# Output projection of a two-layer hybrid trunk: inputs and weight loaded earlier, three input slots, a new order of small steps

## The chip, the cores and the metric

The kernel runs on one core of one Trainium2 chip. The metric is the device time of one launch in microseconds, the median of several executions. All data are float32.

## The reference

A trunk of two layers is applied to 128 prompt rows and 1024 sample rows (1152 rows of 1024 features, nine tiles of 128 rows). One layer is:

```
xm   = rms_norm(x) * (1 + sc1) + sh1
proj = xm @ w_in                       # queries, keys, gates of three mixers
o    = concat(attention, gated linear attention, gated delta rule)
       # forward + backward scan, rms_norm per head * gain, times silu(z)
y    = o @ w_out                       # the output projection
x    = x + g1 * rms_norm(y, nrm1)
xm   = rms_norm(x) * (1 + sc2) + sh2
aff  = softmax(xm @ w_router)          # 16 experts, expert choice
x    = x + g2 * rms_norm(experts(xm, aff))
```

The change is about the lines from `y` to `aff`, and about how the stage ahead of them (the scans and the attention) ends.

## The kernel before, in words

The program is a chain of stages, and each stage ends with a barrier over all engines: `front` (projection by w_in, keys, convolution), `scan` (the two scans and the attention, interleaved by hand), `mixer_output` (output projection, residual, routing), `experts`. Each of the two layers runs all four. SBUF tensors and semaphores belong to a stage; only `B.x`, the masks and a few tables live throughout.

`mixer_output` (L2083) works through nine tiles, software pipelined, each engine with its own loop over t. For tile t:

- SP loads the three parts of the heads' output and the gates (`load(t)`, L2123) into one of two slots, and stores the normalised rows (L2150). Ahead of the loop it issues tile 0, the 4 MB of w_out in four pieces (L2135), tile 1, the branch gates, the residual rows of three tiles at a time (L2142) and w_router.
- DVE, `head_sums` (L2287 to L2292): forward plus backward, squares, sums per head, times z. `head_norms` (L2298 to L2302): times the gain, times the scale per head, which POOL works out (L2168, L2170) in between. The gain is scaled once (L2363) as soon as it has landed.
- PE, `turn_o` (L2224): eight transposes into the two halves of `ring`; ACT copies each half to `oT` (L2211). `project` (L2247): 16 products of 128 x 512 into `acc`; the trace shows each as two records.
- ACT, `branch_square` (L2192) sums the squares of `acc`; POOL makes the scale; DVE, `residual` (L2326, L2328) adds the branch to x; ACT, `row_square` (L2202); POOL; DVE, `normalise` (L2336) writes `xhat`.
- PE, `turn_x` (L2236): eight transposes of `xhat` into the same two halves of `ring`; DVE, `modulate` (L2311): eight products with scale and shift from `ring` to `xT`, four for each half. PE, `route` (L2256): the products with w_router, 16 columns wide, into the one bank `lg`. DVE, `largest` (L2341, L2343): the row maximum of `lg`, negated; ACT, the exponential (L2205); DVE, `affinity` (L2348 to L2354); PE and DVE turn it (L2262, L2376).

Two things set the order around the change. First, `ring` is shared: `turn_o(t)` waits for each half until `modulate(t - 3)` has read it. Second, each engine runs its program in order. PE's order in one pass of its loop is

```
for t in range(-3, TILES + 3):
    if t in (-2, -1): project(t + 2)
    if t >= 1 and has(t + 1): project(t + 1)
    if has(t - 3): turn_affinity(t - 3)
    if has(t): turn_x(t)
    if has(t - 1): route(t - 1)
    if has(t + 3): turn_o(t + 3)
```

and DVE's order in one pass is modulate(t-1), residual(t), head_sums(t+3), normalise(t), head_norms(t+3), largest(t-2), affinity(t-2), copy of affinity t-3. So modulate(t-1) follows turn_x(t-1), and largest(t-2) follows route(t-2); both of these stand in PE's pass t-1, route behind turn_x.

In `scan`, the last values of the delta rule's inverse are used by `values` (L1258). After that come four steps of the state, each with attention between, while SP only stores results (L1094). At that time the tensors Rk, TT, PM, NB, Tb and qk are no longer read.

Of the kernel before, what the change touches and what calls it, by code (L numbers as in the profile page):

```python
# [22 lines left out]
P = 128  # L23
# [153 lines left out]
def front(nc, T, B, l):  # L177
# [32 lines left out]
    with stage(nc, "front", l) as st:  # L210
        keysT, values = st.sb("keysT", [P, H_MLA, KEYS * P]), st.sb("values", [P, H_MLA, KEYS, VD])
        xmT = st.sb("xmT", [P, KD, ROWS])
        w = st.sb("w", [P, 2, KD, 512])
# [6 lines left out]
        wc = st.sb("wc", [P, 2, 3, 512])  # L220
# [713 lines left out]
CH = 64  # L934
# [4 lines left out]
def scan(nc, T, B, l):  # L939
# [30 lines left out]
    with stage(nc, "scan", l) as st:  # L970
        beta, la = st.sb("beta", [P, 2, 32]), st.sb("la", [P, 2, 32])
        qk = st.sb("qk", [P, 4, 2 * DQ])
        v = st.sb("v", [P, 2, 4, H, GK])
        Rk = st.sb("Rk", [P, 32, GK])
        kend = st.sb("kend", [P, 2, 32, GK])
        kq = st.sb("kq", [P, 3, 16, P])
        PM = st.sb("PM", [P, 32, CH])
        A = st.sb("A", [P, 2, 32, CH])
        TT = st.sb("TT", [P, 32, CH])
        nwT = st.sb("nwT", [P, 2, 2, 8, CH])  # L980
        NB = st.sb("NB", [P, 32, 32])
        Tb = st.sb("Tb", [P, 32, 32])
# [53 lines left out]
        s_out = st.sem("s_out")  # L1036
# [11 lines left out]
        with st.block() as block:  # L1048
            @block.sync
            def _(sp):  # L1050
# [70 lines left out]
                load_v(1)  # L1121
                for k in range(-1, GROUPS):
# [959 lines left out]

def mixer_output(nc, T, B, l):  # L2083
# [3 lines left out]
    with stage(nc, "mixer", l) as st:  # L2087
        wout = st.sb("wout", [P, KD, D])
# [3 lines left out]
        o = st.sb("o", [P, 2, D])  # L2092
        ob, z = st.sb("ob", [P, 2, W3]), st.sb("z", [P, 2, W3])
# [12 lines left out]
        c_in, w_in, r_in, gate_in = (st.sem(x) for x in ("c_in", "w_in", "r_in", "gate_in"))  # L2106
        t_in, stored = ([st.sem(f"{x}{i}") for i in range(2)] for x in ("t_in", "stored"))
# [12 lines left out]
        with st.block() as block:  # L2120
            @block.sync
            def _(sp):
                def load(t):  # L2123
                    s, r = t % 2, t * P
                    q = proj_row(t)
                    if t >= 2:
                        sp.wait_ge(o_p, 2 * (t - 2) + 3)
                    for dst, src in ((o[:, s, 0:256], T["mla_out"][r:r + P, :]), (o[:, s, 256:], T["scan_f"][r:r + P, :]), (ob[:, s], T["scan_b"][r:r + P, :]),
                                     (z[:, s, 0:GQ], T["proj"][q:q + P, C_GZ:C_DQ]), (z[:, s, GQ:], T["proj"][q:q + P, C_DZ:C_DB])):
# [11 lines left out]
                for g in range(3):  # L2141
                    sp.dma_start(B.x[:, 3 * g:3 * g + 3, :], xs[:, 3 * g:3 * g + 3, :]).then_inc(x_in[g], 16)  # L2142
                    if g < 2:
                        load(g + 2)
                    if g == 0:
                        sp.dma_start(wr[:], T["w_router"][l].rearrange("(k p) n -> p k n", p=P)).then_inc(r_in, 16)
                for t in range(0, TILES):
                    if t >= 0:
                        sp.wait_ge(xhat_v, t + 2)
                        sp.dma_start(T["xhat"][t * P:(t + 1) * P, :], xhat[:, t % 2]).then_inc(stored[t % 2], 16)  # L2150
                    if 2 <= t + 4 < TILES:
                        load(t + 4)
# [33 lines left out]
            def _(act):  # L2186
# [6 lines left out]

                for t in range(-3, TILES + 2):
# [19 lines left out]
            def _(pe):  # L2214
                def turn_o(t):
                    pe.wait_ge(o_v, t + 2)
                    for i in range(2):
# [4 lines left out]
                        for k in range(4):  # L2222
                            c = (4 * i + k) * P
                            mm = pe.transpose(ring[:, i, k, :], o[:, t % 2, c:c + P], B.ident)  # L2224
# [38 lines left out]

                for t in range(-3, TILES + 3):
# [14 lines left out]
            def _(dve):  # L2279
# [3 lines left out]
                def head_sums(t):  # L2283
                    s = t % 2
# [608 lines left out]
```

## Time and profile before

| | us |
|---|---|
| median of three runs | 4474.08 |
| lowest and highest run | 4464.86, 4477.98 |
| the profiled execution, its own time | 4473.7 |
| its span | 4471.9 |
| output projection stage, layer 0, first instruction to last product of affinity | 1140.7 to 1343.3 |
| the same, layer 1 | 3339.1 to 3541.5 |

Times in rows are microseconds from the start of the span. A row of a timeline gives start, duration, engine, line, operation, what it writes and reads, and in brackets how long the engine was idle before and what it waited for. PE rows of one kind that follow one another are drawn together (x32), and ends of matmuls are modelled. PE is TensorE's product, PEld its weight load, DVE VectorE, ACT ScalarE, POOL GpSimd; a name with q (SPq, ACTq) is the issue of a transfer. PEclk is the clock that TensorE was granted: 1.00 is 2.4 GHz, 0.50 is 1.2 GHz.

### The profile page before, as it was taken

How to read it: one execution, taken by the hardware profiler on the slowest of the kernel's cores; microseconds unless marked ns; L12 is line 12 of the kernel's file. 1: busy time of each engine (PE TensorE's matmuls, PEld its weight loads, DVE VectorE, ACT ScalarE, POOL GpSimd, SP SyncE). 2: the span in 40 equal slices, each digit the busy share in tenths (PEclk: the TensorE clock that was granted, in tenths of full speed). 3: DMA queues.
4: the chain of work that ended last, by engine and by line, in shares of the span. 5: the costliest groups of instructions: out<-in, count | busy, mean ns of one | idle time of the engine just before them, and what ended most of it. 6: DMA issues, size and time to landing. Idle time of an engine off the chain costs nothing. (4 is left out here: it accounts for less than half of the span.)

```text
span 4471.9 us, 80289 instructions
## 1 busy us (share of the span) xinstructions
PE 3865.3 (86%) x33620; PEld 3008.3 (67%) x33620; DVE 2161.6 (48%) x4904; ACT 973.8 (22%) x1962; POOL 1057.2 (24%) x1092
## 2 busy tenths in 40 slices
PE   4999968888795999999779998787869689999994
PEld 3444546676455999999744444566654389999994
DVE  3335045656455445544453440556646554445444
ACT  2233134444110000000033331444431100000001
POOL 0036034453220110001040450454522100110003
PEclk9999978888897999999989998888889789999997
DMA  7556353331516888888564652334224378888885
GB/s 265 170 189 245 128 129 77 80 69 36 182 68 235 296 279 283 283 292 291 173 231 152 242 195 64 95 82 97 53 74 168 117 254 280 294 280 283 284 289 174
DMA packets 557877, 836.17 MB, mean 187 GB/s; under 512 B 85864, under 2 KB 403368, under 8 KB 551372
## 3 DMA queue, kind: packets, MB, share of 16 engines
q1 hardware_dynamic: 471884, 711.08, 49.0%
q10 hardware_dynamic: 70432, 81.03, 5.4%
q0 software_dynamic: 15200, 38.94, 3.5%
q8 instruction: 266, 4.36, 0.4%
q14 instruction: 95, 0.78, 0.1%
HBM read 698.83 MB, written 132.10 MB: 186 GB/s over the span
## 5 line engine op out<-in xcount | busy, mean ns | idle before, releaser
L2545 PE MATMUL ffn_hb<-ffn_xT,ffn_w 128*128 128x144 f32 x8192 | 1058.9, 289 | 26.8 <-DMA ffn_w<-in_w_e 20.3
L2545 PEld LDWEIGHTS ffn_hb<-ffn_xT,ffn_w 128*128 128x128 f32 x8192 | 1029.5, 192 | 29.0 <-DMA ffn_w<-in_w_e 20.5
L521 PE MATMUL front_acc<-front_w,front_xmT 128*128 128x512 f32 (+2 forms) x2304 | 883.5, 544 | 21.3 <-DVE front_xmT L782 17.7
L521 PEld LDWEIGHTS front_acc<-front_w,front_xmT 128*128 128x128 f32 x2304 | 441.2, 194 | 449.5 <-issue 418.1
L2553 PE MATMUL ffn_acc<-ffn_hT,ffn_w 128*128 128x144 f32 x4096 | 547.3, 287 | 0.0
L2553 PEld LDWEIGHTS ffn_acc<-ffn_hT,ffn_w 128*128 128x128 f32 x4096 | 518.5, 190 | 6.7 <-issue 6.7
L2592 ACT ACTIVATE ffn_en<-ffn_hb 128x144 f32<-128x144 f32 x256 | 74.3, 290 | 1457.1 <-PE ffn_hb L2545 1457.1
L2475 POOL DMA_INDIRECT ffn_xe<-scratch_xhat,ffn_g_idx x34 | 34.4, 1012 | 1453.6 <-DVEq L2657 1399.1
L2702 DVE TENSOR_TENSOR ffn_hT<-ffn_en,ffn_hb 128x144 f32<-128x144 f32 x256 | 77.8, 304 | 607.6 <-ACT ffn_en L2592 607.2
L2247 PE MATMUL mixer_acc<-mixer_wout,mixer_oT 128*128 128x512 f32 x576 | 256.4, 604 | 3.2 <-DMA mixer_wout<-in_w_out 1.7
L2618 DVE TENSOR_SCALAR_CACHE_REDUCE ffn_junk<-ffn_row,ffn_pair 128x128 f32<-128x128 f32 (+2 forms) x324 | 245.3, 757 | 1.4
L1798 POOL TENSOR_TENSOR scan_prod<-scan_Tb,scan_NB 128x30 f32<-128x30 f32 (+5 forms) x300 | 181.6, 605 | 222.0 <-POOLq L1815 199.3
L2247 PEld LDWEIGHTS mixer_acc<-mixer_wout,mixer_oT 128*128 128x128 f32 x576 | 110.8, 195 | 136.7 <-issue 132.3
L591 POOL TENSOR_TENSOR x_res<-x_res,front_wc 128x1536 f32<-128x1536 f32 x18 | 72.1, 4003 | 550.6 <-DMA x_res<-scratch_proj 550.6
L2617 DVE TENSOR_SCALAR_CACHE_REDUCE ffn_junk<-ffn_row,ffn_pair 128x128 f32<-128x128 f32 (+6 forms) x252 | 187.2, 743 | 4.4
L1351 PE MATMUL scan_ring<-x_res 128*128 128x512 f32 (+1 forms) x400 | 160.0, 533 | 12.1 <-ACT x_res L1655 4.5
L1800 POOL TENSOR_TENSOR scan_Tb<-scan_Tb,scan_prod 128x30 f32<-128x30 f32 (+5 forms) x300 | 163.1, 544 | 23.5
L1962 DVE TENSOR_REDUCE scan_top<-x_res 128x1 f32<-128x1152 f32 (+1 forms) x72 | 88.7, 1232 | 146.1 <-ACT x_res L1659 127.8
L1332 PE MATMUL scan_ring<-x_res 128*128 128x64 f32 x1168 | 141.1, 275 | 0.9 <-ACT x_res L1682 0.9
L1332 PEld LDWEIGHTS scan_ring<-x_res 128*128 128x128 f32 x1168 | 138.7, 195 | 1.4 <-ACT x_res L1682 1.2
L1351 PEld LDWEIGHTS scan_ring<-x_res 128*128 128x128 f32 x400 | 68.7, 198 | 96.9 <-ACT x_res L1655 48.2
L649 ACT ACTIVATE front_out<-front_acc 128x512 f32<-128x512 f32 (+1 forms) x90 | 49.7, 552 | 386.1 <-PE front_acc L521 386.1
(332 smaller groups left out, 5108.8 us busy)
## 6 DMA issues: line engine op xcount, KB each, us to landing
ffn_w<-in_w_e SPq DMA_DIRECT2D x384, 1024.0 KB, 9.4
x_res<-in_w_mod SPq DMA_DIRECT2D x40, 1024.0 KB, 5.5
x_res<-scratch_proj SPq DMA_DIRECT2D x36, 768.0 KB, 6.1
scratch_proj<-front_out ACTq DMA_DIRECT2D x90, 256.0 KB, 2.2
ffn_row<-scratch_affT SPq DMA_DIRECT2D x36, 576.0 KB, 4.5
front_w<-in_w_in ACTq DMA_DIRECT2D x8, 2048.0 KB, 13.2
scan_qk<-scratch_qkv SPq DMA_DIRECT2D x16, 1024.0 KB, 9.9
scratch_qkv<-x_res SPq DMA_DIRECT2D x18, 768.0 KB, 3.5
```

The source lines that it names most:

```text
L521: mm = pe.matmul(acc[:, U % 2, 0:size], xmT[:, k, t * P:(t + 1) * P], w[:, n % 2, k, 0:size], start=k == 0, stop=k == KD - 1)
L1332: mm = pe.matmul(b[:, P:P + VD], probT[:, k * P:(k + 1) * P], kv[:, h % 2, KEYS_W + (j0 + k) * VD:KEYS_W + (j0 + k + 1) * VD], start=k == ...
L1351: mm = pe.matmul(ring[:, i % 2, 0:size], qT[:, n % 4, :], kv[:, h % 2, k0 + at:k0 + at + size], start=True, stop=True)
L1798: pool.tensor_tensor(x, wide(Tb[:, 0:i, i], n), NB[:, i + 1:32, i].unsqueeze(1).to_broadcast([P, i, n]), ALU.mult).then_inc(own, step())
L1800: pool.tensor_tensor(Tb[:, 0:i, i + 1:32], Tb[:, 0:i, i + 1:32], x, ALU.add).then_inc(own, step())
L1962: dve.tensor_reduce(top[:, c], prob[:, n % 2, 0:w], AX.X, ALU.max).then_inc(own, step())
L2247: mm = pe.matmul(acc[:, t % 2, n * 512:(n + 1) * 512], oT[:, t % 2, k, :], wout[:, k, n * 512:(n + 1) * 512], start=k == 0, stop=k == KD - 1)
L2545: mm = pe.matmul(hb[:, b, i * CAP:(i + 1) * CAP], w[:, r, k, c:c + P], xT[:, s, k, :], start=k == 0, stop=k == KD - 1)
L2553: mm = pe.matmul(part(c), w2[:, r, j % WIDTH, c * P:(c + 1) * P], hT[:, b, :], start=j == 0 and c % PER_BANK == 0, stop=j == KF - 1, skip_ ...
L2617: dve.tensor_scalar(junk[:, 0:a - lo], row[:, lo:a], mine, 0.0, ALU.is_ge, ALU.add, accum_out=counts[:, t, 0:1]).then_inc(own, step())
L2618: dve.tensor_scalar(junk[:, a - lo:hi - lo], row[:, a:hi], mine, 0.0, ALU.is_gt, ALU.add, accum_out=counts[:, t, 1:2]).then_inc(own, step())
L2702: dve.tensor_tensor(hT[:, b, :], en[:, b], hb[:, b, CAP:2 * CAP], ALU.mult).then_inc(h_done, 1)
```

## The change

- Two SBUF tensors live throughout the program: `B.late` (8192 numbers a partition) and `B.early` (4096). The weight slots of `front` and Rk, TT, PM, NB, Tb of `scan` move into `B.late`; `wc` of front and `qk` of scan into `B.early`. In `mixer_output`, `wout` is `B.late`, and the first of three input slots is `B.early`.
- SP issues the five loads of tile 0 and the four of w_out in `scan`, ahead of the stores of the last group, once PE has made the last `values`. The scan's SP waits for them at its end.
- `load(t)` has three slots: tiles 1 and 2 are issued at the stage's begin, tile t+5 behind the store of tile t.
- PE begins the stage with nine products of constants, 128 x 512 each, into `acc`.
- ACT: the row square of tile 0 stands in pass -1, ahead of the copies of tile 2.
- DVE: `largest` stands at the head of the pass, ahead of `modulate`; the sums of tile 0 stand ahead of the wait for the gain; the scaling of the branch gates stands at the end of pass -1 and no longer in residual(0).
- PE's loop (the order given above) is not touched.

```
+                def load_next():
+                    sp.wait_ge(head_out[0], 17)
...
+                    sp.wait_ge(od_out[0], 33)
+                    sp.wait_ge(od_out[1], 33)
+                    sp.wait_ge(og_out[0], 33)
+                    sp.wait_ge(u_p, 10)
+                    o, ob, z = mixer_inputs(B)
+                    q = proj_row(0)
+                    for dst, src in ((o[:, 0:256], T["mla_out"][0:P, :]), (o[:, 256:], T["scan_f"][0:P, :]), (ob, T["scan_b"][0:P, :]),
+                                     (z[:, 0:GQ], T["proj"][q:q + P, C_GZ:C_DQ]), (z[:, GQ:], T["proj"][q:q + P, C_DZ:C_DB])):
+                        sp.dma_start(dst, src).then_inc(next_in, 16)
+                    wo = T["w_out"][l].rearrange("(k p) n -> p k n", p=P)
+                    for i in range(0, KD, 2):
+                        sp.dma_start(B.late[:].rearrange("p (k n) -> p k n", k=KD)[:, i:i + 2], wo[:, i:i + 2]).then_inc(next_in, 16)
                 for k in range(-1, GROUPS):
                     g = k + 1
+                    if g == GROUPS:
+                        load_next()
                     if k >= 0:
                         for m in range(2):
                             store_gdn(k, m)
...
                 sp.wait_ge(s_out, 129)
+                sp.wait_ge(next_in, 16 * 9 + 1)
...
+def mixer_inputs(B):
+    return B.early[:, 0:D], B.early[:, D:D + 768], B.early[:, D + 768:D + 2 * 768]
...
-        wout = st.sb("wout", [P, KD, D])
+        wout = B.late[:].rearrange("p (k n) -> p k n", k=KD)
-        o = st.sb("o", [P, 2, D])
-        ob, z = st.sb("ob", [P, 2, W3]), st.sb("z", [P, 2, W3])
+        o, ob, z = ([x, more[:, 0], more[:, 1]] for x, more in zip(mixer_inputs(B), (
+            st.sb("o", [P, 2, D]), st.sb("ob", [P, 2, W3]), st.sb("z", [P, 2, W3]))))
...
-                    s, r = t % 2, t * P
+                    s, r = t % 3, t * P
-                    if t >= 2:
-                        sp.wait_ge(o_p, 2 * (t - 2) + 3)
+                    if t >= 3:
+                        sp.wait_ge(o_p, 2 * (t - 3) + 3)
...
-                load(0)
-                wo = T["w_out"][l].rearrange("(k p) n -> p k n", p=P)
-                for k in range(0, KD, 2):
-                    sp.dma_start(wout[:, k:k + 2], wo[:, k:k + 2]).then_inc(w_in, 16)
                 load(1)
+                load(2)
...
-                        load(g + 2)
+                        load(g + 3)
...
-                    if 2 <= t + 4 < TILES:
-                        load(t + 4)
+                    if t + 5 < TILES:
+                        load(t + 5)
...
+                def row_square(t):
+                    act.wait_ge(x_v, t + 2)
+                    act.activation(sq[:, 1], B.x[:, t, :], ACT.Square, accum_out=rs[:, t % 2, 1:2]).then_inc(x_a, 1)
                 for t in range(-3, TILES + 2):
                     s = t % 2
                     if t == -1:
                         branch_square(0)
-                    if has(t):
-                        if t:
-                            branch_square(t)
-                        act.wait_ge(x_v, t + 2)
-                        act.activation(sq[:, 1], B.x[:, t, :], ACT.Square, accum_out=rs[:, s, 1:2]).then_inc(x_a, 1)
+                        row_square(0)
+                    if t >= 1 and has(t):
+                        branch_square(t)
+                        row_square(t)
...
                 def project(t):
                     pe.wait_ge(oT_a, 2 * t + 3)
-                    if t == 0:
-                        pe.wait_ge(w_in, 65)
...
+                for _ in range(9):
+                    pe.matmul(acc[:, 1, 0:512], B.ident, B.masks[:].rearrange("p k c -> p (k c)"), start=True, stop=True)
...
+                def branch_gates():
+                    dve.wait_ge(gate_in, 49)
+                    for c in range(2):
+                        dve.scalar_tensor_tensor(gate[:, c, :], gate[:, c, :], float(D) ** 0.5, ygain[:], ALU.mult, ALU.mult).then_inc(own, step())
...
                 for t in range(-3, TILES + 4):
+                    if has(t - 2):
+                        largest(t - 2)
                     if has(t - 1):
                         modulate(t - 1)
                     if has(t):
                         residual(t)
+                    if has(t + 3):
+                        head_sums(t + 3)
                     if t == -3:
                         dve.wait_ge(c_in, 33)
                         dve.tensor_scalar(gain[:], gain[:], float(GK) ** 0.5, None, ALU.mult).then_inc(own, step())
-                    if has(t + 3):
-                        head_sums(t + 3)
                     if has(t):
                         normalise(t)
                     if has(t + 3):
                         head_norms(t + 3)
-                    if has(t - 2):
-                        largest(t - 2)
+                    if t == -1:
+                        branch_gates()
                     if has(t - 2):
                         affinity(t - 2)
...
+        B.late, B.early = sb("late", [P, 2 * KD * 512]), sb("early", [P, 4 * D])
```

## Rows read from the trace of the kernel before

**Rows 1.** The page's first part: busy time and share of the span by engine

```profile
PE 3865.3 (86%) x33620; PEld 3008.3 (67%) x33620; DVE 2161.6 (48%) x4904; ACT 973.8 (22%) x1962; POOL 1057.2 (24%) x1092
```

**Rows 2.** Busy time by stretch of layer 0's stage: length, engines, clock, DMA, GB/s

```profile
1140.80:1156.90 16.10, 0.00 (x0) 0.00 (x0) 6.05 (x9) 0.00 (x0) 3.35 (x3) 0.50 0.87 323
1156.90:1163.60 6.70, 5.84 (x13) 3.40 (x14) 0.59 (x1) 1.19 (x2) 0.00 (x0) 0.50 1.04 401
...
1217.60:1322.60 105.00, 104.12 (x383) 56.55 (x382) 62.87 (x128) 21.19 (x46) 25.34 (x32) 1.00 0.21 73
```

**Rows 3.** Timeline, the stage's begin in layer 0, up to its first projection

```profile
1140.81 0.09 DVE L2281 MEMSET mixer_af<- 128x36 f32 x1 [5.96 <-PEq L104]
...
1147.26 0.23 DVE L2363 TENSOR_SCALAR mixer_gain<-mixer_gain 128x128 f32<-128x128 f32 x1 [6.37 <-DMA mixer_gain<-in_gdn_out_norm]
...
1149.36 0.96 DVE L2287 TENSOR_TENSOR mixer_o<-mixer_o,mixer_ob 128x768 f32<-128x768 f32 x1 [1.87 <-DMA mixer_z<-scratch_proj]
...
1156.91 1.97 PE L2224 MATMUL mixer_ring<-masks_sb,mixer_o 128*128 128x128 f32 x8 [22.67 <-DVE mixer_o L2302]
...
1159.73 15.96 PE L2247 MATMUL mixer_acc<-mixer_wout,mixer_oT 128*128 128x512 f32 x32 [0.86 <-DMA mixer_wout<-in_w_out]
```

**Rows 4.** Timeline, from the second projection's end to the third

```profile
1191.14 1.04 PE L2224 MATMUL mixer_ring<-masks_sb,mixer_o 128*128 128x128 f32 x8
...
1195.77 1.97 PE L2236 MATMUL mixer_ring<-masks_sb,mixer_xhat 128*128 128x128 f32 x8 [3.60 <-DVE mixer_xhat L2336]
...
1200.71 2.30 PE L2224 MATMUL mixer_ring<-masks_sb,mixer_o 128*128 128x128 f32 x8 [2.96 <-DVE mixer_xT L2311]
1201.90 0.60 ACT L2211 ACTIVATE mixer_oT<-mixer_ring 128x512 f32<-128x512 f32 x1 [7.94 <-PE mixer_ring L2224]
1202.80 14.84 PE L2247 MATMUL mixer_acc<-mixer_wout,mixer_oT 128*128 128x512 f32 x32
```

**Rows 5.** Timeline, one steady pass between two projections

```profile
1235.75 2.64 DVE L2311 TENSOR_SCALAR mixer_xT<-mixer_ring,scale,shift 128x128 f32<-128x128 f32 x8 [0.16 <-PE mixer_ring L2236]
...
1235.91 1.86 PE L2256 MATMUL mixer_lg<-mixer_wr,mixer_xT 128*128 128x16 f32 x16
...
1238.44 0.66 PE L2224 MATMUL mixer_ring<-masks_sb,mixer_o 128*128 128x128 f32 x4 [0.19 <-DVE mixer_xT L2311]
...
1238.94 13.90 PE L2247 MATMUL mixer_acc<-mixer_wout,mixer_oT 128*128 128x512 f32 x32
```

**Rows 6.** Timeline, the stage's end in layer 0, behind the last projection

```profile
1323.39 1.86 PE L2256 MATMUL mixer_lg<-mixer_wr,mixer_xT 128*128 128x16 f32 x16
1325.78 1.27 DVE L2326 SCALAR_TENSOR_TENSOR mixer_branch<-mixer_acc,mixer_rs,mixer_gate 128x1024 f32<-128x1024 f32 x1
...
1333.06 3.43 PE L2256 MATMUL mixer_lg<-mixer_wr,mixer_xT 128*128 128x16 f32 x16
1336.53 0.17 DVE L2341 TENSOR_REDUCE mixer_mx<-mixer_lg 128x1 f32<-128x16 f32 x1 [1.14 <-PE mixer_lg L2256]
...
1337.44 3.57 PE L2256 MATMUL mixer_lg<-mixer_wr,mixer_xT 128*128 128x16 f32 x16 [0.73 <-ACT mixer_ex L2205]
```

**Rows 7.** Busy time by stretch where the granted clock falls, stays down and rises

```profile
1325.40:1327.50 2.10, 0.00 (x0) 0.00 (x0) 2.07 (x4) 0.00 (x0) 0.00 (x0) 1.00 0.00 0
1327.50:1331.30 3.80, 0.00 (x1) 0.00 (x1) 1.63 (x3) 1.15 (x2) 0.79 (x2) 0.51 0.00 0
1331.30:1342.00 10.70, 9.19 (x42) 8.61 (x42) 5.06 (x23) 1.09 (x6) 0.00 (x0) 0.50 0.12 49
1387.10:1392.20 5.10, 5.09 (x21) 5.09 (x22) 4.92 (x17) 0.00 (x0) 0.00 (x0) 0.50 0.00 0
```

**Rows 8.** The scan's last part (timeline), and the weight's transfers (KB each, us to landing)

```profile
1094.16 2.08 PE L1258 MATMUL scan_pA<-scan_v,scan_TT 64*64 64x64 f32 x64 [0.19 <-ACT scan_v L1603]
...
1134.59 0.26 DVE L1974 TENSOR_SCALAR x_res<-x_res,scan_rden 128x64 f32<-128x64 f32 x1 [3.19 <-issue]
...
mixer_wout<-in_w_out SPq DMA_DIRECT2D x4, 1024.0 KB, 11.6
```

More of the change, by code:

```diff
@@ L212, in front @@
         xmT = st.sb("xmT", [P, KD, ROWS])
-        w = st.sb("w", [P, 2, KD, 512])
+        w = B.late[:].rearrange("p (s k n) -> p s k n", s=2, k=KD)
         out = st.sb("out", [P, 3, 512])
@@ L219, in front @@
         ss, yss, power = st.sb("ss", [P, TILES]), st.sb("yss", [P, TILES]), st.sb("power", [P, TILES])
-        wc = st.sb("wc", [P, 2, 3, 512])
+        wc = B.early[:, 0:6 * 512].rearrange("p (s j n) -> p s j n", s=2, j=3)
         hss = st.sb("hss", [P, 3 * H_GDN])
@@ L971, in scan @@
         beta, la = st.sb("beta", [P, 2, 32]), st.sb("la", [P, 2, 32])
-        qk = st.sb("qk", [P, 4, 2 * DQ])
+        qk = B.early[:].rearrange("p (m c) -> p m c", m=4)
         v = st.sb("v", [P, 2, 4, H, GK])
-        Rk = st.sb("Rk", [P, 32, GK])
+        Rk, TT, PM = (B.late[:, i * 2048:(i + 1) * 2048].rearrange("p (b e) -> p b e", e=CH) for i in range(3))
+        NB, Tb = (B.late[:, i * 1024:(i + 1) * 1024].rearrange("p (b c) -> p b c", c=32) for i in (6, 7))
         kend = st.sb("kend", [P, 2, 32, GK])
         kq = st.sb("kq", [P, 3, 16, P])
-        PM = st.sb("PM", [P, 32, CH])
         A = st.sb("A", [P, 2, 32, CH])
-        TT = st.sb("TT", [P, 32, CH])
         nwT = st.sb("nwT", [P, 2, 2, 8, CH])
-        NB = st.sb("NB", [P, 32, 32])
-        Tb = st.sb("Tb", [P, 32, 32])
         prod = st.sb("prod", [P, 256])
@@ L2105, in mixer_output @@
         lg, at = st.ps("lg", [P, 512]), st.ps("at", [P, 512])
-        c_in, w_in, r_in, gate_in = (st.sem(x) for x in ("c_in", "w_in", "r_in", "gate_in"))
-        t_in, stored = ([st.sem(f"{x}{i}") for i in range(2)] for x in ("t_in", "stored"))
+        c_in, r_in, gate_in = (st.sem(x) for x in ("c_in", "r_in", "gate_in"))
+        t_in, stored = [st.sem(f"t_in{i}") for i in range(3)], [st.sem(f"stored{i}") for i in range(2)]
         x_in = [st.sem(f"x_in{g}") for g in range(3)]
@@ L2147, in _ @@
                 for t in range(0, TILES):
[L2148 to L2152 removed]
+                    sp.wait_ge(xhat_v, t + 2)
+                    sp.dma_start(T["xhat"][t * P:(t + 1) * P, :], xhat[:, t % 2]).then_inc(stored[t % 2], 16)
+                    if t + 5 < TILES:
+                        load(t + 5)
                 sp.wait_ge(at_v, TILES + 1)
@@ L2283, in head_sums @@
                 def head_sums(t):
[L2284 to L2287 removed]
+                    s = t % 3
+                    m = o[s][:, 256:]
+                    if t:
+                        dve.wait_ge(t_in[s], 80 * ((t if s else t - 3) // 3) + 81)
+                    dve.tensor_tensor(m, m, ob[s], ALU.add).then_inc(own, step())
                     dve.wait_ge(own, step.n)
[L2289 removed]
+                    dve.tensor_tensor(ob[s], m, m, ALU.mult).then_inc(own, step())
                     dve.wait_ge(own, step.n)
[L2291 to L2292 removed]
+                    dve.tensor_reduce(ss[:, t % 2], ob[s].rearrange("p (h e) -> p h e", e=GK), AX.X, ALU.add).then_inc(heads_v, 1)
+                    dve.tensor_tensor(m, m, z[s], ALU.mult).then_inc(own, step())
                 def head_norms(t):
[L2295 to L2296 removed]
+                    mh = o[t % 3][:, 256:].rearrange("p (h e) -> p h e", e=GK)
                     dve.wait_ge(own, step.n)
@@ L2316, in residual @@
                     if t == 0:
-                        dve.wait_ge(gate_in, 49)
-                        for c in range(2):
-                            dve.scalar_tensor_tensor(gate[:, c, :], gate[:, c, :], float(D) ** 0.5, ygain[:], ALU.mult, ALU.mult).then_inc(own, step())
                         dve.wait_ge(own, step.n)
```

21 lines of the change are left out of this document (8 added, 13 removed).

## The prediction, made before the changed kernel ran

> **What bounds the kernel now.** The page comes first: PE is busy 86% of the span [rows 1], and stages are fenced by barriers. So a change to one stage is worth what it takes off that stage's own chain, twice, once a layer; layer 1's stage repeats layer 0's row for row, 2198.4 us later. I then cut layer 0's stage into stretches. The table shows three kinds. For 16.1 us PE does nothing: it waits for the first tile [rows 2]. Then it works at the 1.2 GHz level for 6.7 us [rows 2]. From the third projection's end to the last one's it is busy 104.1 of 105.0 us at 2.4 GHz [rows 2]: there PE's program order is the bound and nothing can be won, only lost. Two more holes are seen in the timeline: between the second and third projection [rows 4] and behind the last [rows 6].
>
> **The loads moved into the scan** cost nothing, I think. They are released when PE has made the last values, at 1096.3, and the scan's last DVE step ends at 1134.85 [rows 8]: 38 us. A piece of w_out took 11.6 us to land with all four in flight [rows 8], and the five inputs are a third of its bytes, so all is in SBUF by about 1115. What SP has queued behind the nine issues are the stores of the last group, of which the first is due ten microseconds later; a store may land late behind the 4 MB, and two steps on DVE would wait for its buffer. If this cover fails I bound the price at 3 us a layer (below: nothing, since the scan cannot end earlier). The semaphores, the wait at the scan's end and the moved tensors: 0.
>
> **The stage's begin.** Today DVE's first sum starts at 1149.36, PE's first turn at 1156.91: a chain of 7.55 us [rows 3]. With tile 0 in place the chain starts at 1140.9 and would end at 1148.4. The gain lands at 1147.26 [rows 3] and comes into this chain now; behind it stand two products and the last one of the chain, so the turn could start by 1149.6 or so. The nine constant products then decide. One projection is 32 records in 13.90 us, 0.434 us a record [rows 5]; nine products are 18 records, 7.8 us at 2.4 GHz and 15.6 us at 1.2. How long does the low clock last once PE works? 6.7 us here [rows 2], 5.1 us at the experts' begin [rows 7]. With 5.1 us low: 5.9 records, then 12.1 x 0.434 = 5.3 us, in all 10.4 us; with 6.7 us low 11.2. I take 10.4, the row with PE busy throughout: the turn starts at 1151.3. Turn to projection took 2.8 us with the turns at 1.97 us; the turns take 1.04 at full clock [rows 3, 4], so 1.9. Projection 0 runs 1153.2 to 1167.1, against 1175.69 today [rows 3]: **8.6 us won**.
>
> **Between the second and third projection** today 11.5 us pass [rows 4]: PE waits 3.6 us for xhat(0), since the branch gates and the row square come late, then 2.96 us for modulate(0). Now the gates are scaled in pass -1 and the row square stands ahead of the copies of tile 2, so both are done during the second projection (if residual(0) were late, ACT would hold the copies of tile 2, and PE the third projection; by my count residual(0) ends some 9 us before they are due). What is left from the end E of the projection: half a turn 0.5, two copies of 0.6 [rows 4], the second half of turn_x at E + 2.2; modulate takes 2.64 [rows 5], from E + 1.8 to E + 4.4; the last half turn 0.5. The third projection starts at E + 4.9, and finds the high clock, 13.90 in place of 14.84 [rows 4, 5]: 11.5 + 14.84 - 4.9 - 13.90 = **7.5 us won**. With the 8.6: 16.1 us a layer, 32.2 in all.
>
> **What the new order on DVE costs.** This is the part that looks harmless. largest(t-2) needs route(t-2), and PE makes that behind turn_x(t-1). modulate(t-1) needs only turn_x(t-1). In the rows modulate runs beside route: it starts at 1235.75 while route runs to 1237.77 and ends at 1238.39; PE's half turn at 1238.44 waits for it by 0.19 us only, and the projection starts at 1238.94 [rows 5]. With largest in front, DVE stands until route's end R = 1237.77, takes 0.35 us for the maximum and its sign, and only then starts 2.64 us of modulate: half done at R + 1.7, all at R + 3.0. PE turns one half, idles, turns the other, and starts the projection at R + 3.5, not R + 1.17. That is 2.35 us a pass, in the five passes where turn_o(4) to turn_o(8) follow: **11.8 us lost** a layer, 23.6 in all. Nothing covers it, since PE has no idle time there [rows 2].
>
> At the end the same exchange counts twice. modulate(7) waits for route(6), which ends at 1325.25; it ended at 1325.8 today, with residual(8) right behind [rows 6], and would end at 1328.2: 2.4 us. Then largest(7) at 1336.53 [rows 6] stands ahead of modulate(8), which today is done before it: modulate(8) ends 3.0 us behind it, at 1339.5 on today's scale, and route(8) starts then, not at 1337.44: 2.1 us. Together 4.5 us a layer, **9.0** in all.
>
> **The clock.** Between route and the projection PE would now have 1.7 us idle, half a turn of 0.5, 0.8 idle, half a turn. Where PE ran dry at 1325.4 the clock was 1.00 for 2.1 us and 0.5 from then on [rows 7]. And route itself does not count as full work: with PE busy 9.2 of 10.7 us, mostly on it, the clock stayed at 0.50 [rows 7]. So from turn_x's end to the projection there are 5.3 us with one microsecond of full-width work in them. Nothing in the trace shows just this. The lower bound is 0: no single gap reaches 2.1 us. The upper is a restart like projection 0, 15.96 against 13.90, 2.1 us; a milder one is 14.84 against 13.90, 0.9 us [rows 3, 4, 5]. It is nearer to a drop than to none, as today's gap behind turn_o(2), after which the clock was down, holds about as much work; I take 1.5 us for each of ten restarts, **15 us**, and keep 0 and 21 as ends. The Trainium skill ("TensorE: Matmul & The Clock Gate", section "HAM oscillation — how this bites in real kernels") speaks against this change in the same way: a loop whose gap throws the clock back pays the transition in each pass. By its rule of thumb, which asks for one idle gap of a certain length, these gaps would be too short and the sum 15 us smaller, 4474; the rows of a falling clock here come after 2.1 us of idle time, and no run shows a broken gap.
>
> **The sum.** 4473.7 - 32.2 + 23.6 + 9.0 + 15 = 4489.1. The profiled time, 4473.7 (span 4471.9), is within 0.4 us of the median of the runs, so this is also the forecast for the median: **4489 us**. No change, as far as a measurement of this kernel tells, is within 0.3%, 13.4 us: 4460.7 to 4487.5.
>
> **Rivals.**
> - The clock holds through the broken gaps (20%): 4474. For it: no gap reaches 2.1 us. Against: how little work lies around them.
> - The order on DVE costs nothing, because largest is released early or modulate keeps its place beside route (8%): then 32.2 us are won and nothing is given back, 4442. This is the other side. It is decided at one place: the start of L2311 against the end of L2256 in the steady passes; below a delay of 0.4 us a pass the kernel is faster by more than the bound. Against it: DVE's rows are in program order throughout.
> - The constant products run cold to their end (10%): 15.6 us, not 10.4, so the turn starts at 1156.5 and 5.2 us less are won a layer: 4499. For it: they start on a PE that has stood idle since the scan. Against: every stretch of 512-column products in the trace reached the high clock within 6.7 us.
> - The change doesn't do what its title says: "routing products behind the turns" is already the order of PE's loop, and the diff leaves that loop alone. Had route moved behind turn_o too, the wait on DVE would be longer still. This adds no number; it is why I price the order as read in the diff.
> - The scan's end is held by the loads (2%): up to 6 us more, 4495.
>
> **How the numbers follow.** The forecast with its clock price between 0.9 and 2.1 us, and 2 us a layer either way in the begin, spans 4479 to 4499 and has 60%. Some two thirds of it lie above 4487.5 (0.40), the rest is "same". The cold constants and a held scan add 0.12 to slower. The holding clock gives 0.18 same and 0.02 faster, the harmless order 0.07 faster and 0.01 same. So slower 0.52, same 0.39, faster 0.09. The range of 8 in 10 takes in the forecast's span, most of the holding clock and of the cold constants, and leaves out the harmless order: 4468 to 4504.
>
> **What would show each step.** In the changed profile: w_out's transfers near 1097, landed before 1120, and the scan's end at 1134.85 as today; DVE's first sum at 1141; 18 records of constants ending near 1151, the first real projection near 1153; the third starting about 34.7 us after it. In the steady passes L2341 ahead of L2311 with a wait on L2256, L2311 starting about 2.3 us later behind turn_x, PE idle about 2.4 us before its two half turns, and a period of 20 to 22 us, not 17.75. PEclk below 1.00 at the head of most projections would bear out the clock price; 1.00 throughout would refute it. A period still at 17.75 would refute the main step, and a time under 4460 with it.

## The result, and the profile after

The changed kernel takes 4484.7 us (median of 20 runs, 4477.5 to 4495.0) against 4472.1 us for the kernel before in the same session (20 runs, 4462.0 to 4479.8). The ratio is 1.0029, with a 95% interval of 1.0022 to 1.0037: **12.6 us slower**. The runs resolve this difference, but it lies just inside the 0.3% that the prediction called no change. The forecast was 4489, its range 4468 to 4504. Two executions, one of the kernel before (5642.5 us) and one of experiment 4 (4759.0 us), ran at a lower granted clock (0.69 and 0.84, in the others 0.92 to 0.93) and are in no median or ratio here.

The page's first part, and one group of its fifth, for the kernel after (engine busy us, share, instructions; then line, engine, operation, output and inputs, count, busy us, mean ns of one):

```profile
PE 3884.2 (87%) x33656; PEld 3010.7 (67%) x33656; DVE 2149.9 (48%) x4904; ACT 973.2 (22%) x1962; POOL 1059.8 (24%) x1092
...
L2268 PE MATMUL mixer_acc<-late,mixer_oT 128*128 128x512 f32 x576 | 262.8, 616 | 3.0 <-ACT mixer_oT L2234 3.0
```

PE's busy time rose by 18.9 us against [rows 1], and by 36 records, which are the constant products. DVE, ACT and POOL issue the same instructions as before.

In layer 0 the stage begins at 1137.96 and the next one at 1353.64: 215.7 us, where the kernel before took 207.6. Layer 1 has 215.8 and 207.4. So the stage lost 8.1 and 8.3 us, **16.4 in all**. Three cuts of it show where. The beginning, as a timeline (start, duration, engine, line, operation, output and inputs, count, in brackets the idle time before and what ended it):

```profile
1138.01 10.62 PE L2286 MATMUL mixer_acc<-masks_sb 128*128 128x512 f32 x18 [6.54 <-PEq L104]
...
1138.05 0.95 DVE L2311 TENSOR_TENSOR early<-early 128x768 f32<-128x768 f32 x1
...
1144.38 0.23 DVE L2392 TENSOR_SCALAR mixer_gain<-mixer_gain 128x128 f32<-128x128 f32 x1 [2.54 <-DMA mixer_gain<-in_gdn_out_norm]
...
1145.70 0.96 DVE L2325 TENSOR_TENSOR early<-early,mixer_ss 128x768 f32<-128x768 f32 x1
...
1148.46 1.04 PE L2247 MATMUL mixer_ring<-masks_sb,early 128*128 128x128 f32 x8
...
1150.23 14.00 PE L2268 MATMUL mixer_acc<-late,mixer_oT 128*128 128x512 f32 x32 [0.74 <-ACT mixer_oT L2234]
...
1183.30 0.63 PE L2247 MATMUL mixer_ring<-masks_sb,early 128*128 128x128 f32 x4 [1.11 <-DVE mixer_xT L2334]
1184.49 0.66 PE L2247 MATMUL mixer_ring<-masks_sb,early 128*128 128x128 f32 x4 [0.56 <-DVE mixer_xT L2334]
1184.98 13.90 PE L2268 MATMUL mixer_acc<-late,mixer_oT 128*128 128x512 f32 x32
```

DVE's first sum starts at once, where it waited 8.6 us [rows 3]. Tile 0 is ready at 1146.66, but PE is on its constants until 1148.63. Projection 0 ends 26.3 us behind the stage's begin; before it was 35.0 [rows 3]. The third projection ends 60.9 us behind it, before 76.9 [rows 4]: 16.0 us are won here.

One pass in the middle, PE's and DVE's rows of the timeline:

```profile
1223.14 0.17 DVE L2366 TENSOR_REDUCE mixer_mx<-mixer_lg 128x1 f32<-128x16 f32 x1 [4.51 <-PE mixer_lg L2277]
1223.35 0.15 DVE L2368 TENSOR_SCALAR mixer_mx<-mixer_mx 128x1 f32<-128x1 f32 x1
1223.43 2.64 DVE L2334 TENSOR_SCALAR mixer_xT<-mixer_ring,scale,shift 128x128 f32<-128x128 f32 x8
...
1224.95 0.79 PE L2247 MATMUL mixer_ring<-masks_sb,mixer_o 128*128 128x128 f32 x4 [1.84 <-DVE mixer_xT L2334]
1226.13 1.11 PE L2247 MATMUL mixer_ring<-masks_sb,mixer_o 128*128 128x128 f32 x4 [0.39 <-DVE mixer_xT L2334]
1227.04 14.72 PE L2268 MATMUL mixer_acc<-late,mixer_oT 128*128 128x512 f32 x32
```

DVE stands 4.51 us until route has ended, takes the maximum, and only then begins modulate. In [rows 5] DVE waited 0.16 us for turn_x and began modulate while route ran. PE idles 1.84 and 0.39 us ahead of its two half turns, which take 0.79 and 1.11 us, not 0.6, and the projection takes 14.72, not 13.90: part of this runs at the low clock. The busy time by stretch says the same (stretch, length, busy time of PE, PEld, DVE, ACT and POOL, granted clock, DMA share, GB/s):

```profile
1199.00:1309.50 110.50, 99.60 (x348) 55.13 (x346) 56.19 (x112) 19.13 (x42) 24.60 (x30) 0.91 0.15 54
1222.50:1226.90 4.40, 2.17 (x14) 1.71 (x14) 2.90 (x10) 0.60 (x1) 0.00 (x0) 0.81 0.00 0
1226.90:1230.00 3.10, 3.10 (x7) 1.38 (x6) 0.06 (x1) 1.60 (x3) 0.79 (x2) 0.71 0.00 0
1230.00:1243.00 13.00, 13.00 (x42) 6.43 (x40) 9.42 (x14) 1.40 (x4) 4.77 (x4) 1.00 0.41 134
```

The clock was 1.00 throughout these passes before [rows 2]; now its mean is 0.91. Five such passes follow one another; their projections take 15.45, 14.72, 15.99, 14.93 and 14.40 us, and they start 20.1 to 22.6 us apart, not 17.75. From the third projection's end to the last one's 124.6 us pass, before 104.9 [rows 2]: 19.6 us are lost here.

The stage's end, PE's rows:

```profile
1324.26 1.86 PE L2277 MATMUL mixer_lg<-mixer_wr,mixer_xT 128*128 128x16 f32 x16
...
1334.53 1.97 PE L2259 MATMUL mixer_ring<-masks_sb,mixer_xhat 128*128 128x128 f32 x8 [8.29 <-DVE mixer_xhat L2361]
1336.29 3.44 PE L2277 MATMUL mixer_lg<-mixer_wr,mixer_xT 128*128 128x16 f32 x16
...
1342.75 3.59 PE L2277 MATMUL mixer_lg<-mixer_wr,mixer_xT 128*128 128x16 f32 x16 [2.81 <-DVE mixer_xT L2334]
```

The last route waits 2.81 us for modulate; it waited 0.73 for the exponential before [rows 6]. From the end of the last projection to the next stage's begin it is 30.2 us, not 25.7: 4.5 us lost. The sum: -16.0 + 19.6 + 4.5 = +8.1, the measured difference of layer 0.

**Outside the stage** nothing got longer by more than 1.9 us (layer 1's `experts`, 927.3 us against 925.3, and between 924.7 and 928.2 in all ten profiles). The loads were issued in the scan at 1093.25 to 1098.3, their first and last rows being

```profile
1093.25 0.32 SPq L1133 DMA_DIRECT2D early<-scratch_mla_out  x1
...
1095.58 2.74 SPq L1136 DMA_DIRECT2D late<-in_w_out  x4
```

and layer 0's scan lasted 566.7 us, against 569.7 before. The spans of the two profiled executions differ by 7.2 us only, not 16.4, mainly since this scan took 3.0 us less in the changed kernel and layer 1's `front` 7.2 us less, 536.0 us against 543.2. In the profile of before PE stood there 3.56 us on ACT, and the granted clock has a mean of 0.83 in the twenty microseconds around it. That stage's length lay between 532.8 and 544.4 us over the ten kernels profiled here, and layer 1's scan between 563.9 and 572.2. The two kernels with the old tensors (before, and experiment 2) have the two longest `front` stages, 543.2 and 544.4, but the next is 541.7, so one profile of each tells little. So the **stage's own length** is the sharper measure of an edit, and the medians differ from the sum over the two stages by up to 4.8 us either way.

### The profile page after: what moved, and what is told of

Same layout as the page of the kernel before. It is cut to its first block and busy times, and to the rows that moved or that the text cites. A ratio compares the mean times of both kernels' runs of the same rounds, so it can differ in the third digit from the quotient of the medians.

```text
span 4479.1 us, 80373 instructions
## 1 busy us (share of the span) xinstructions
PE 3884.2 (87%) x33656; PEld 3010.7 (67%) x33656; DVE 2149.9 (48%) x4904; ACT 973.2 (22%) x1962; POOL 1059.8 (24%) x1092
## 5 line engine op out<-in xcount | busy, mean ns | idle before, releaser
L521 PE MATMUL front_acc<-late,front_xmT 128*128 128x512 f32 (+2 forms) x2304 | 879.8, 541 | 17.7 <-DVE front_xmT L782 17.7
L521 PEld LDWEIGHTS front_acc<-late,front_xmT 128*128 128x128 f32 x2304 | 438.8, 193 | 444.6 <-issue 417.4
L2268 PE MATMUL mixer_acc<-late,mixer_oT 128*128 128x512 f32 x576 | 262.8, 616 | 3.0 <-ACT mixer_oT L2234 3.0
L1817 POOL TENSOR_TENSOR scan_prod<-late 128x30 f32<-128x30 f32 (+5 forms) x300 | 183.8, 613 | 222.3 <-POOLq L1834 199.6
L2268 PEld LDWEIGHTS mixer_acc<-late,mixer_oT 128*128 128x128 f32 x576 | 113.6, 200 | 140.6 <-issue 136.7
L591 POOL TENSOR_TENSOR x_res<-x_res,early 128x1536 f32<-128x1536 f32 x18 | 75.6, 4202 | 545.2 <-DMA x_res<-scratch_proj 545.2
L2644 DVE TENSOR_SCALAR_CACHE_REDUCE ffn_junk<-ffn_row,ffn_pair 128x128 f32<-128x128 f32 (+6 forms) x252 | 187.2, 743 | 4.4
L1370 PE MATMUL scan_ring<-x_res 128*128 128x512 f32 (+1 forms) x400 | 161.1, 536 | 10.9 <-issue 4.0
L1819 POOL TENSOR_TENSOR late<-late,scan_prod 128x30 f32<-128x30 f32 (+5 forms) x300 | 162.1, 540 | 23.5
```

The costliest lines, as they stand in the source:

```text
L521: mm = pe.matmul(acc[:, U % 2, 0:size], xmT[:, k, t * P:(t + 1) * P], w[:, n % 2, k, 0:size], start=k == 0, stop=k == KD - 1)
L1370: mm = pe.matmul(ring[:, i % 2, 0:size], qT[:, n % 4, :], kv[:, h % 2, k0 + at:k0 + at + size], start=True, stop=True)
L1817: pool.tensor_tensor(x, wide(Tb[:, 0:i, i], n), NB[:, i + 1:32, i].unsqueeze(1).to_broadcast([P, i, n]), ALU.mult).then_inc(own, step())
L1819: pool.tensor_tensor(Tb[:, 0:i, i + 1:32], Tb[:, 0:i, i + 1:32], x, ALU.add).then_inc(own, step())
L2268: mm = pe.matmul(acc[:, t % 2, n * 512:(n + 1) * 512], oT[:, t % 2, k, :], wout[:, k, n * 512:(n + 1) * 512], start=k == 0, stop=k == KD - 1)
L2644: dve.tensor_scalar(junk[:, 0:a - lo], row[:, lo:a], mine, 0.0, ALU.is_ge, ALU.add, accum_out=counts[:, t, 0:1]).then_inc(own, step())
```

## The experiments

The theory: `largest` ahead of `modulate` makes each steady pass wait for route, costs 2.35 us of waiting a pass and the clock besides, and undoes a gain of 16 us a layer that the other parts make. The rivals: the loss comes from elsewhere (the input slots, the loads, the constants), or the clock has no part in it. The first four kernels ran in one session (before: 4469.0 us, 16 runs), the other four in a second one (before: 4474.2, 9 runs).

### 1. `largest` put back

```
                 for t in range(-3, TILES + 4):
-                    if has(t - 2):
-                        largest(t - 2)
                     if has(t - 1):
                         modulate(t - 1)
...
                     if has(t + 3):
                         head_norms(t + 3)
+                    if has(t - 2):
+                        largest(t - 2)
```

> The changed kernel with largest(t-2) back at its old place on DVE, behind head_norms; all else as changed. Theory A (the loads, the constants and the early gates win about 16 us a layer; largest ahead of modulate gives them back, half by the wait on route, half by the clock that falls in the longer gap): the steady passes are back at 17.75 us, the stage takes about 191.5 us, not 215.7 as changed or 207.5 before, and the time is about 32 us under the kernel before, near 4440. Rival B (the steady passes are long for another reason, the third input slot or the moved tensors): the stage stays near 215 us and the time near 4484. Rival C (the clock falls because the stage now runs at another phase, and would do so with any order): passes near 18.5 to 19 us and a time near 4450.

4436.7 us (6 runs), ratio 0.9927 [0.9915, 0.9939]: **32.4 us faster than before**, and some 45 us faster than the change as it stands. The stage takes 192.0 and 191.8 us. One pass, PE's rows, and the stretch of the steady passes:

```profile
1216.45 1.04 PE L2259 MATMUL mixer_ring<-masks_sb,mixer_xhat 128*128 128x128 f32 x8
1217.33 1.86 PE L2277 MATMUL mixer_lg<-mixer_wr,mixer_xT 128*128 128x16 f32 x16
1219.03 0.63 PE L2247 MATMUL mixer_ring<-masks_sb,mixer_o 128*128 128x128 f32 x4
1219.86 0.66 PE L2247 MATMUL mixer_ring<-masks_sb,mixer_o 128*128 128x128 f32 x4 [0.19 <-DVE mixer_xT L2334]
```

```profile
1198.00:1300.00 102.00, 101.11 (x375) 55.15 (x374) 62.97 (x129) 21.23 (x46) 25.34 (x32) 1.00 0.19 68
```

The idle time of 0.19 us is that of [rows 5], the clock is 1.00, and the projections of these passes take 13.90 us. Two lines of order carry the whole loss. From the third projection's end to the last one's it is 104.9 us in both layers, the same as before: the third input slot wins nothing in the steady passes. The whole gain stands ahead of them, at the stage's begin and between the second and third projection.

### 2. `largest` first, alone, in the kernel before

The same two lines, moved the other way in the kernel before.

> The kernel before with that one edit alone: largest(t-2) at the head of DVE's pass, ahead of modulate(t-1). Theory A: the five passes with a turn_o become 20.1 us plus 0.5 to 2 us of clock each, the stage's end 4.4 us longer: the stage 207.5 + 19.6 + 4.4 = 231.5 us, the whole 4472 + 48 = 4520. Rival B: no more than 4480.

4519.4 us (4 runs), ratio 1.0112 [1.0097, 1.0127]: 50.4 us slower. The stage takes 231.6 and 232.3 us, 24.0 and 24.9 more than before; the prediction's steps for this order (11.8 + 4.5 + 7.5) make 23.8 a layer. A pass of it:

```profile
1214.54 1.04 PE L2236 MATMUL mixer_ring<-masks_sb,mixer_xhat 128*128 128x128 f32 x8
1215.41 1.86 PE L2256 MATMUL mixer_lg<-mixer_wr,mixer_xT 128*128 128x16 f32 x16
1219.09 2.30 PE L2224 MATMUL mixer_ring<-masks_sb,mixer_o 128*128 128x128 f32 x8 [1.82 <-DVE mixer_xT L2311]
```

The cost is there without the slots, the early loads and the constants. With the first experiment this settles the cause: one edit, done alone and undone alone, gives the same amount, 48.9 us in the two stages here and 47.7 between the change and the first experiment.

### 3. The gap filled with work

Nothing is waited for less; PE gets products of constants to do while it waits. This is work that the output doesn't need.

```
+                def fill(n):
+                    pe.matmul(at[64:128, 128:128 + n], B.ident[:, 64:128], B.masks[:].rearrange("p k c -> p (k c)")[:, 0:n], start=True, stop=True)
...
                         for k in range(4):
...
                         mm.then_inc(o_p, 1)
+                        if t >= 4 and i == 0:
+                            fill(256)
...
                         route(t - 1)
+                        if t <= 5:
+                            fill(384)
+                            fill(384)
+                            fill(256)
```

> The changed kernel with PE kept busy in the gap that the order on DVE opens: behind route in passes 1 to 5 three products of constants (384, 384 and 256 columns, about 1.7 us, into 64 partitions of the bank at that nothing reads), and one of 256 columns between the two half turns. Theory A: the waits stay, so each pass keeps its 2.35 us, but the clock holds at 1.00, each projection takes 13.9 us instead of 14.4 to 16.0, and the kernel gets about 7 us a layer shorter than changed: near 4471. If the clock had no part in it (the long projections come from transfers or from the weight's place), the projections stay at 14.4 to 16.0 us and the time at 4484 or a little over.

4473.6 us (12 runs), ratio 1.0010 [1.0001, 1.0019]. The stage takes 208.1 and 206.7 us, where the change has 215.7 and 215.8: 7.6 and 9.0 us less, with more work and no wait taken away. A pass:

```profile
1200.84 1.94 PE L2239 MATMUL mixer_at<-masks_sb 128*64 128x384 f32 x6
1202.73 0.64 PE L2250 MATMUL mixer_ring<-masks_sb,mixer_o 128*128 128x128 f32 x4
1203.29 0.65 PE L2239 MATMUL mixer_at<-masks_sb 128*64 128x256 f32 x2
1203.91 0.66 PE L2250 MATMUL mixer_ring<-masks_sb,mixer_o 128*128 128x128 f32 x4
1204.40 13.90 PE L2273 MATMUL mixer_acc<-late,mixer_oT 128*128 128x512 f32 x32
```

```profile
1198.00:1301.00 103.00, 103.00 (x389) 55.36 (x387) 56.19 (x112) 19.11 (x42) 24.56 (x30) 1.00 0.17 60
```

The period is now 20.0 to 20.1 us in all five passes. From the third projection's end to the last one's it is 116.7 us in both layers, 11.8 more than before: five waits of 2.35. The other 7.8 us of the 19.6 were **the clock**, 6.0 in the projections and 1.8 in the turns ahead of them. (The 9.0 us of layer 1 hold 1.2 more, since the nine constants at the begin took 9.50 us there and 10.66 in the changed kernel.) The rival without a clock price falls. The medians show less of it: against the kernel before, each in its own session, the change has +12.6 us and this kernel +4.6, so 8.0 us are won, where the two stages have 16.6 and I expected 14. In the profile layer 1's scan took 572.2 us, 8.1 more than in the changed kernel; no run tells whether that belongs to the edit.

### 4. The branch gates and the row square as before

Without `largest` first, the part of the change that closed the second gap is taken back.

```
                     if t == -1:
                         branch_square(0)
-                        row_square(0)
-                    if t >= 1 and has(t):
-                        branch_square(t)
+                    if has(t):
+                        if t:
+                            branch_square(t)
                         row_square(t)
...
                     if t == 0:
+                        branch_gates()
                         dve.wait_ge(own, step.n)
...
-                    if t == -1:
-                        branch_gates()
```

> The kernel of e1_largest_back with two more edits undone: the branch gates scaled in residual(0), and the row square of tile 0 in pass 0 behind the copies of tile 2. Theory A: xhat(0) is late again, PE waits for it and for modulate(0) and finds the low clock: 7 us a layer longer than e1_largest_back, so near 4454 if that is at 4440. Rival: the inputs now come so early that the gates are not late in either order, and only the row square counts: 3 to 4 us a layer, near 4447.

4453.5 us (5 runs), ratio 0.9967 [0.9954, 0.9980], 16.9 us more than the first experiment. PE's rows between second and third projection:

```profile
1186.19 1.97 PE L2259 MATMUL mixer_ring<-masks_sb,mixer_xhat 128*128 128x128 f32 x8 [3.60 <-DVE mixer_xhat L2362]
1191.13 2.30 PE L2247 MATMUL mixer_ring<-masks_sb,early 128*128 128x128 f32 x8 [2.97 <-DVE mixer_xT L2334]
```

Both waits of [rows 4] are back, with their lengths. The stage is 5.7 and 7.8 us longer; in layer 0 the constants happened to take 1.6 us less in this profile (9.36 us), so that part alone is about 7.3, forecast 7.5. The two edits were undone together, so how the 7.3 divides between gates and row square is not shown.

### 5. No constant products

`for _ in range(9)` becomes `range(0)`, in the kernel of the first experiment.

> The kernel of e1_largest_back without the nine constant products at the stage's begin. In that run the first turn waits for the constants: 18 records of 11.0 us, while DVE has tile 0 ready 8.6 us after the stage's begin. Without them the turn starts 2 us earlier but at the low clock: 1.97 us of turns in place of 1.04, and a first projection of 15.9 instead of 14.0. Theory A: about 1 us a layer longer, 2 us in all, not to be told from e1_largest_back by the time, only by the rows. Rival (the constants are worth a real share of the 8.7 us of the begin): 4 us or more a layer.

4441.4 us (5 runs), ratio 0.9925 [0.9912, 0.9939]. The stage takes 192.9 and 193.3 us, 1.0 and 1.6 more than with them, near the 1 us of theory A. PE's first rows:

```profile
1147.20 1.97 PE L2247 MATMUL mixer_ring<-masks_sb,early 128*128 128x128 f32 x8 [15.26 <-DVE early L2325]
1149.86 16.21 PE L2268 MATMUL mixer_acc<-late,mixer_oT 128*128 128x512 f32 x32 [0.69 <-ACT mixer_oT L2234]
```

The constants save 0.93 us of the turn and 2.21 of projection 0, and give two thirds of it back, since nine of them end 2 us behind the tile's being ready.

### 6. The loads back at the stage's begin

Again in the kernel of the first experiment; the semaphore `w_in` with its wait in `project(0)` and the wait of `head_sums` for tile 0 return too.

```
-                def load_next():
...
-                    if g == GROUPS:
-                        load_next()
...
-                sp.wait_ge(next_in, 16 * 9 + 1)
...
+                load(0)
+                wo = T["w_out"][l].rearrange("(k p) n -> p k n", p=P)
+                for k in range(0, KD, 2):
+                    sp.dma_start(wout[:, k:k + 2], wo[:, k:k + 2]).then_inc(w_in, 16)
                 load(1)
```

> The kernel of e1_largest_back with the loads of tile 0 and of w_out back at the stage's begin (three slots, constants and the order of the small steps as there; the weight still in the long-lived tensor). Theory A: the first sum waits 8.6 us again, the constants end while PE still has nothing to do, the clock falls once more, and the first projection ends some 8.7 us later; gates and row square stay early if their transfers, now queued behind 5 MB, come in time, else the second hole opens again. So 9 us a layer longer than e1_largest_back, up to 13: 4454 to 4463. Rival: the constants keep the clock and 2 us of this are saved: 7 us a layer.

4456.6 us (5 runs), ratio 0.9961 [0.9947, 0.9975]. The stage takes 200.2 and 200.1 us, 8.2 and 8.4 more, a little under the 9 of theory A. PE's first rows:

```profile
1137.81 10.73 PE L2270 MATMUL mixer_acc<-masks_sb 128*128 128x512 f32 x18 [6.61 <-PEq L104]
1154.15 1.97 PE L2229 MATMUL mixer_ring<-masks_sb,early 128*128 128x128 f32 x8 [5.61 <-DVE early L2308]
1156.85 15.76 PE L2252 MATMUL mixer_acc<-late,mixer_oT 128*128 128x512 f32 x32 [0.73 <-ACT mixer_oT L2216]
```

With tile 0 late, the same constants are worth nothing: PE idles 5.61 us behind them, and the turn and projection 0 run about as slowly as before [rows 3], so the rival in which they keep the clock falls. The early loads are what carries the begin; the constants are an addition to them.

### 7. The stage's end filled

In the kernel of the first experiment, seven more constant products stand where PE waits for the last xhat.

```
+                    if t == TILES - 1:
+                        pe.wait_ge(acc_v, t + 1)
+                        for _ in range(7):
+                            pe.matmul(acc[:, 1, 0:512], B.ident, B.masks[:].rearrange("p k c -> p (k c)"), start=True, stop=True)
                     if has(t):
                         turn_x(t)
```

> The kernel of e1_largest_back with seven products of constants (512 columns) on PE ahead of turn_x(8), where PE waits some 6 us for the last xhat and the clock falls. If the clock is what makes the stage's end slow: turn_x(8) 1.04 instead of 1.97 us, route(7) and route(8) 1.9 instead of 3.4 and 3.6 us, so up to 4 us a layer, 8 in all, near 4429. If the clock falls again at once, since route is weak work, only turn_x and route(7) gain: 2 us a layer.

4435.7 us (5 runs), ratio 0.9920 [0.9905, 0.9935]. The stage takes 190.4 us in both layers, 1.6 and 1.4 less. PE's rows at the end in the first experiment, then in this one, and this one's granted clock:

```profile
1312.72 1.97 PE L2259 MATMUL mixer_ring<-masks_sb,mixer_xhat 128*128 128x128 f32 x8 [5.94 <-DVE mixer_xhat L2361]
1314.49 3.43 PE L2277 MATMUL mixer_lg<-mixer_wr,mixer_xT 128*128 128x16 f32 x16
```

```profile
1305.22 6.17 PE L2297 MATMUL mixer_acc<-masks_sb 128*128 128x512 f32 x14
1311.32 1.09 PE L2259 MATMUL mixer_ring<-masks_sb,mixer_xhat 128*128 128x128 f32 x8
1312.25 1.86 PE L2277 MATMUL mixer_lg<-mixer_wr,mixer_xT 128*128 128x16 f32 x16
...
1316.23 3.45 PE L2277 MATMUL mixer_lg<-mixer_wr,mixer_xT 128*128 128x16 f32 x16 [2.00 <-ACT mixer_ex L2228]
```

```profile
1312.00:1316.00 4.00, 2.23 (x21) 2.02 (x19) 3.51 (x14) 0.28 (x2) 0.00 (x0) 1.00 0.32 131
1316.00:1327.00 11.00, 4.03 (x18) 3.48 (x18) 2.12 (x11) 0.45 (x3) 0.02 (x1) 0.52 0.03 8
```

The turn and the first route run at full clock, in 1.09 and 1.86 us, not 1.97 and 3.43. But the last route waits longer for the exponential, 2.00 us, where it waited 0.73. The clock is still 1.00 at the end of this wait and falls just as the route begins, so that route is slow again (3.45 us; in layer 1 3.27). This is the second case of what I expected, 2 us a layer, and not the 4 us of the first.

### 8. Seven constants at the begin, not nine

`range(9)` becomes `range(7)` in the kernel of experiment 7.

> The kernel of e7_filled_end with seven constant products at the stage's begin in place of nine. They end 1.7 us earlier, about when DVE has tile 0 ready (8.6 us after the begin), so the first turn starts 1.5 to 2 us earlier a layer at the high clock: 3 to 4 us in all. If the clock has not yet risen by then, nothing or a loss of 1 us a layer.

4431.7 us (5 runs), ratio 0.9909 [0.9895, 0.9923], the **fastest of all**: the stage takes 187.2 and 188.9 us, 3.2 and 1.5 less than in experiment 7.

```profile
1138.86 8.96 PE L2286 MATMUL mixer_acc<-masks_sb 128*128 128x512 f32 x14 [6.54 <-PEq L104]
1147.66 1.08 PE L2247 MATMUL mixer_ring<-masks_sb,early 128*128 128x128 f32 x8
1149.48 5.85 PE L2268 MATMUL mixer_acc<-late,mixer_oT 128*128 128x512 f32 x13 [0.74 <-ACT mixer_oT L2234]
```

The first turn starts 8.8 us behind the stage's begin (9.0 in layer 1), in experiment 7 10.7 and 10.8, and finds the clock high all the same: 1.8 us a layer are the constants' part, as expected. Over all profiles nine constants let the turn start 9.2 to 10.9 us behind the begin where tile 0 is there. Between this kernel and the seventh the medians' intervals overlap; the stage's length and these rows show the difference. The rest of it is the last route, which took 2.02 us in layer 0 and 3.56 in layer 1, and no run shows that this follows from the edit; it accounts for most of the distance between 187.2 and 188.9.

## Why the prediction was right

**The loads in the scan** cost nothing, as forecast: issued at 1093 to 1098, the scan not longer. The rival of a held scan falls.

**The stage's begin.** Forecast: 8.6 us won; measured 8.7. The constants took 10.62 us for 10.4. The turn started 10.5 us behind the begin of the stage, as the sum had it (1151.3 on the scale of before, where the stage begins at 1140.8). I had put the gain's landing at its old time, 6.5 us behind the stage's begin; it landed at 6.4. The nine constants took between 9.4 and 11.0 us in the twelve stages profiled with them, and never ran at the low clock to their end, which would be 15.6: the rival of 10% falls.

**Between second and third projection.** The third starts 34.75 us behind the first. The prediction's list of signs says 34.7, but its own terms add up to 34.4: the gap between second and third came out at 5.1 us, not the 4.9 of the sum. Won by then in both parts: 16.0, forecast 16.1.

**The order on DVE** is the step that decided, and it came as read from the order of the program: five passes with 2.35 us each, forecast 11.8, by experiment 3 11.8. The stage's end: forecast 4.5, measured 4.5.

**The clock** was the one term that no row gave. I took 1.5 us a restart, 7.5 a layer; measured 7.8 (6.0 in the projections, 1.8 in what stands ahead of them). That a drop comes was reasoned from rows; that its price came out so close is partly luck, for 1.5 was the middle of 0.9 and 2.1, and the five projections lost unlike amounts, 0.5 to 2.1 us. The rival in which the broken gap leaves the clock alone (20%) falls by the granted clock of 0.81 and 0.71 and by experiment 3. The rule in the Trainium skill ("TensorE: Matmul & The Clock Gate", section "HAM oscillation — how this bites in real kernels") was right in its warning, a price paid in every pass; its rule of thumb, one idle gap of a certain length, would have spared these gaps of 1.84 and 0.39 us, and the measurement decides against it.

**The sum.** By the terms the stage should lose 15.4 us over both layers; it lost 16.4; 0.6 of the difference is the clock's term. The median moved by 12.6. The 4 us between 16.4 and 12.6 are not found in the stage; no experiment tells whether they are scatter or a small gain elsewhere, and this stays open. It is also why the likeliest class was missed by a hair: I gave 0.52 to slower by over 0.3% and 0.39 to no change, and the ratio is 1.0029, with the bound inside its interval. The range and the mechanism held; a sum that lands 2 us above a bound should have had its chances nearer to even. The step that made them uneven is the "two thirds" above 4487.5: of an even spread from 4479 to 4499 it is 0.57, which gives 0.47 for slower and 0.44 for no change.

**What I did not look for** in the prediction is how cheaply the loss was to be had back. The change holds 32 us of gain, and two lines of order give away 45.

## What to carry to other kernels

When a step is moved to the head of an engine's pass, ask what it waits for and what now stands behind it: here 0.3 us of DVE work with a late producer held back what stood behind it, and through it PE by 2.35 us in each pass. Where TensorE is the bound, price a new wait twice, once as idle time and once for the clock it may cost; if the wait can't be removed, products of constants in it can give the second part back, as in experiment 3. And end such warming work when the real operand is ready, not later: with seven products the first turn started 1.8 us earlier than with nine.

## What the runs showed of the hardware

- The granted clock fell in a stretch where no idle gap was longer than 1.84 us (0.81, then 0.71), with sixteen-column products ahead and half a turn behind that gap. Between second and third projection of the same profile, with idle gaps of 0.41, 1.11 and 0.56 us and full turns ahead of the longest of them, it stayed at 1.00 and the third projection took 13.90 us. The two stretches differ in the longest gap and in the work around it, so they do not show which of the two decides.
- After a wait of 2.00 us the last route took 3.45 and 3.27 us in the two layers of experiment 7, 2.02 and 3.56 in those of experiment 8 (1.86 is its length at 2.4 GHz). In each of the two layer 0 profiles the clock was 1.00 through the wait; in experiment 7 it fell as the route began, in experiment 8 1.7 us later. The same instructions come out either way.
- Filling the waits with products of constants took PE from 99.60 of 110.5 us busy to all of 103.0 of 103.0, and this part of the stage got shorter by 7.8 us in either layer.
